# A fourth of eight weight blocks computed as seven products in each pair of FFN chunks

## The reference, cut to what matters

```
v = rmsnorm(h, ffn_norm_w[l])                                # 256 x 2048
h = h + (silu(v @ w_gate[l]) * (v @ w_up[l])) @ w_down[l]    # w_gate, w_up: 2048 x 5632
```

## Time and profile before

| | us |
|---|---|
| median of 3 runs | 2417.15 (2416.17 to 2417.87) |
| profiled execution, its own time | 2416.8 |
| its span | 2415.0 |
| TensorE busy | 2402.1 (99%) |
| VectorE busy | 1652.5 (68%) |
| ScalarE busy | 1324.2 (55%) |
| mean granted clock of TensorE | 0.998 |
| ffn1's ten pairs | 451.6 to 882.8 in the span |

### The profile page before, as it was taken

How to read it: one execution, slowest core, us unless ns; L and a number is a source line. 1 busy time by engine, 2 the same in 40 slices (tenths; PEclk the granted TensorE clock), 3 DMA queues, 4 the chain that set the end, 5 groups by cost and what they waited for, 6 DMA issues and landing times.

```text
span 2415.0 us, 36120 instructions
## 1 busy us (share of the span) xinstructions
PE 2402.1 (99%) x13287; PEld 2030.0 (84%) x13287; DVE 1652.5 (68%) x2053; ACT 1324.2 (55%) x1691; POOL 47.1 (2%) x105
## 2 busy tenths in 40 slices
PE   9999999999999999999999999999999999999999
PEld 8888888788888888888888888898888888888887
DVE  6478765788888885445668575477777777644465
ACT  5467744555555555444655455466656556444464
POOL 2300000000000000000000000000000000000000
PEclk9999999999999999999999999999999999999999
DMA  8644546566666666556665556655656666666654
GB/s 269 189 142 120 150 166 184 165 201 194 201 189 206 191 205 205 191 191 183 171 188 168 174 143 188 192 184 183 200 183 189 192 192 190 208 194 193 211 195 150
DMA packets 235102, 448.55 MB, mean 186 GB/s; under 512 B 14368, under 2 KB 31604, under 8 KB 234480
## 3 DMA queue, kind: packets, MB, share of 16 engines
q1 hardware_dynamic: 231712, 434.83, 57.8%
q0 software_dynamic: 3280, 12.21, 1.6%
HBM read 443.84 MB, written 3.15 MB: 185 GB/s over the span
## 4 chain that ended last, share of the span: by engine, by line
PE 97%; DVE 1%; ACT 1%; issue 0%; DMA 0%; SPq 0%; DVEq 0%; ACTq 0%
PE pg L2636 15%; PE pg L2638 15%; PE pg L2637 15%; PE pt L3193 7%; PE pg L3193 6%; PE pg L3119 5%; PE pg L3121 5%; PE pg L3120 5%; PE pg L3197 3%; PE pt L3197 3%; PE pg L2695 3%; PE pg L2696 3%; PE pg L2697 3%; PE pt L3119 1%; PE pt L3121 1%; PE pt L3120 1%
## 5 line engine op out<-in xcount | busy, mean ns | idle before, releaser
L1584 DVE TENSOR_TENSOR wlo<-raw,whi 128x1024 fp32r<-128x1024 f32 (+3 forms) x783 | 926.1, 1193 | 652.3 <-ACT whi L756 650.3
L756 ACT ACTIVATE whi<-raw 128x1024 fp32r<-128x1024 f32 (+3 forms) x813 | 834.1, 1033 | 869.6 <-PE pg L2638 544.8
L2636 PE MATMUL pg<-whi,FH 128*128 128x512 f32 x696 | 271.4, 390 | 0.7 <-DVE FL L2081 0.7
L2638 PE MATMUL pg<-whi,FL 128*128 128x512 f32 x696 | 270.9, 389 | 0.0
L2637 PE MATMUL pg<-wlo,FH 128*128 128x512 f32 x696 | 270.8, 389 | 0.0
L3193 PE MATMUL pt<-A,whi 128*128 128x512 f32 x704 | 244.8, 391 | 0.0
L3193 PE MATMUL pg<-A,whi 128*128 128x512 f32 x640 | 222.3, 391 | 0.0
L2636 PE MATMUL pg<-whi,A 128*128 128x512 f32 (+1 forms) x576 | 221.1, 384 | 0.0
L2638 PE MATMUL pg<-whi,A 128*128 128x512 f32 (+1 forms) x576 | 217.7, 378 | 0.0
L2637 PE MATMUL pg<-wlo,A 128*128 128x512 f32 (+1 forms) x576 | 217.5, 378 | 0.0
L3197 PE MATMUL pg<-A,wlo 128*128 128x256 f32 x704 | 197.3, 280 | 0.0
(11 more groups left out here) (602 smaller groups left out, 4077.8 us busy)
## 6 DMA issues: line engine op xcount, KB each, us to landing
raw<-w_up SPq DMA_DIRECT2D x264, 512.0 KB, 4.4
raw<-w_down SPq DMA_DIRECT2D x176, 512.0 KB, 3.7
raw<-w_in SPq DMA_DIRECT2D x151, 512.0 KB, 3.7
raw<-w_gate SPq DMA_DIRECT2D x88, 512.0 KB, 3.7
raw<-w_out SPq DMA_DIRECT2D x64, 512.0 KB, 3.7
raw<-w_ple_gate SPq DMA_DIRECT2D x32, 512.0 KB, 4.4
raw<-w_in SPq DMA_DIRECT2D x32, 388.0 KB, 3.3
raw<-w_in SPq DMA_DIRECT2D x16, 280.0 KB, 3.2
```

Of the source, the lines that this page charges most:

```text
L756: A(whi[:, n % RING, 0:w], raw[:, n % RING, 0:w], ACT.Copy).then_inc(hi_ready, 1)
L1584: V.tensor_tensor(wlo[:, n % RING, 0:w], raw[:, n % RING, 0:w], whi[:, n % RING, 0:w].bitcast(F32), ALU.subtract).then_inc(lo_ready, 1)
L2636: mm(o, xh, wh, start=first and k == 0, stop=False)
L2638: ins = mm(o, xl, wh, start=False, stop=last and k == SK - 1)
```

## The change

Block 5 becomes a block of seven products, so that 4, 5 and 6 are three such blocks in a row. Sixteen small activation sums are made in place of twelve, four differences in place of five, and the combinations are 24 tiles in place of 22. The hooks that make them move to earlier steps of the first pair.

```diff
-SEVEN = (2, 4, 6)
+SEVEN = (2, 4, 5, 6)
 ScalarE:
-            ffn1({2: f1_in(3), 4: norm_ffn1, 6: lambda: take_root(2, D), 14: f1_combos})
+            ffn1({2: f1_in(3), 4: norm_ffn1, 6: lambda: take_root(2, D), 12: f1_combos})
 VectorE:
-            ffn1({2: f1_in(3), 4: norm_ffn1, 6: lambda: rstd(2, D), 9: f1_whole, 10: f1_differences, 12: f1_seven_sums, 15: f1_combos})
+            ffn1({2: f1_in(3), 4: norm_ffn1, 6: lambda: rstd(2, D), 7: f1_whole, 9: f1_differences, 10: f1_seven_sums, 13: f1_combos})
```

## The result

| | before | after |
|---|---|---|
| median | 2417.51 (4 runs) | 2501.02 (2500.43 to 2502.39, 4 runs) |
| ratio to before, 95% interval | | 1.0346 (1.0333 to 1.036) |
| profiled execution, its own time | 2416.8 | 2501.6 |
| its span | 2415.0 | 2499.7 |
| mean granted clock | 0.998 | 0.987 |

The account below looks back on a forecast made before the run. The prediction took TensorE to bound the kernel, busy for 99% of the span. To the profiled 2416.8 us it added -6.8 + 67.6 - 6.0 + 22 = +76.8, giving 2493.6 us, forecast as 2494, range 2463 to 2522.

Parts of the forecast that it names:

- Matmuls removed: Block 5 on TensorE goes from 24 to 21 matmuls in each of 10 pairs, all on the path: -6.8 us.
- The wait of the three in a row: TensorE waits for the shared T set before blocks 5 and 6, 20 times 3.38 us: +67.6 us.
- Start of the pairs: Earlier sums remove the XL gap and slow matmuls, less a new 0.7 us gated-product wait: -6.0 us.
- The clock: Granted clock falls in half of the 20 new TensorE gaps, slowing matmuls behind them: +22 us, ends 0 and +44.
- The clock never falls: Rival 1: the new gaps stay too short to lower the clock, 2471.6 us; chance 0.21.
- In each gap: Rival 2: the clock falls in every one of the new gaps, 2515.6 us; chance 0.19.
- Only one transition stalls: Rival 3: only one of block transitions 4 to 5 and 5 to 6 waits, 2437.8 us, up to 2449; chance 0.06.
- faster: Rival 4: the wait before block 5 is hidden and TensorE does not stop, 2404.0 us; chance 0.03.
- The busy share in the pairs: Sign in the new profile: TensorE's busy share in ffn1 near 87%.
- The slow matmuls: Sign in the new profile: 128x512 matmuls of more than 0.39 us in blocks 5, 6 and 7.

Follow-up runs that it names:

- the kernels with two and three blocks of seven: Against the changed kernel, seven products only in blocks 2 and 4 (2417.7 us) or in 2, 4 and 6 (2412.0 us), hooks early in both.
- Filled gaps: Changed kernel with 12 idle matmuls on TensorE ahead of block 5 and of block 6 in each pair: 2472.73 us, ratio 1.0229.
- scattered sevens: Changed kernel with seven products in blocks 2, 4 and 6 as before, only the hooks at their new, earlier steps: 2412.0 us, ratio 0.9975.
- one pair of neighbours: Changed kernel with seven products in blocks 2, 4 and 5 instead of 2, 4, 5 and 6, hooks early: 2458.87 us, ratio 1.0167.
- the first half gets another home: Changed kernel with the first two weight sums and their low parts alternating between two homes: 2471.93 us, ratio 1.0222.
- when they go back: Changed kernel, four blocks of seven products, with the hooks back at their old steps: 2507.15 us, ratio 1.0365.
- low parts first: Changed kernel with VectorE making the low parts wlo before waiting for the T set, and TensorE's start waiting for these alone: 2436.68 us, ratio 1.008.
- the short filling: Changed kernel with 4 idle matmuls, in place of the filled gaps' 12, ahead of blocks 5 and 6: 2495.7 us, ratio 1.0325.

## Why the prediction was right

Forecast 2494, measured 2501.0, inside 2463 to 2522; the direction and the likeliest case are those forecast.

- *Matmuls removed, -6.8.* Priced at 6.3 us by the kernels with two and three blocks of seven, within some 3 us. Right as far as this can tell; that 240 more matmuls in the gaps cost nothing shows the other side of it, that a matmul counts only where TensorE does not wait.
- *The wait of the three in a row, +67.6.* Twenty waits of 3.1 us, in the line forecast, with restarts 3.29 us late where 3.28 was forecast. Filled gaps less scattered sevens is 2472.7 - 2412.0 = 60.7 us, and that is to be 67.6 - 6.8 = 60.8. The mechanism is shown from four sides: it comes with neighbours and not with work (one pair of neighbours, ten waits), it shrinks by 0.9 us when the first half gets another home, it nearly goes when the low parts are made first, and it does not depend on the clock.
- *Start of the pairs, -6.0.* Measured -6.2 with the hooks alone, and +6.1 when they go back. The wait of 0.7 us on the gated product, counted from the end of the stream, was 0.67.
- *The clock, +22.* Measured 28.3 (2501.0 - 2472.7). This is the one term that I sized too small: I took half of the gaps, which was a choice between two ends and read from no row, and it fell in 13 of 20. The price of a fall, 2.2 us read from the single one before, is met by the mean, 28.3 / 13 = 2.2, but by no fall: six cost 2.7 us and seven 1.5, and that this mix gives the same mean is luck. Where all falls were short, as with one pair of neighbours, the price was 1.5. In the changed kernel the clock mostly falls at the first gap of a pair (9 of 10). Behind each of the six long stretches the second gap was spared (rows above, 1.00 behind 598.69); behind each of the three short ones it was not.
- *The parts together.* -6.2 + 60.7 + 28.3 = 82.8, against 83.5 measured; the difference is that of the two medians of the kernel before, 2418.22 and 2417.51.
- *Rivals.* "The clock never falls" (2471.6) is what the filled gaps made of it, 2472.7: a good number for a kernel that was not this one. "In each gap" (2515.6) falls with the seven gaps without a fall. "Only one transition stalls" and "faster" fall with the 20 waits. The rule of the Trainium skill (TensorE: Matmul & The Clock Gate, "Why this matters for your kernels") that idle gaps between bursts of matmuls bring the clock down, which I had applied to every gap, agrees with the trace in its direction only: 13 of 20.
- *Not forecast.* The busy share in the pairs (87% by full clock) reads 45.14 / 51.38 = 88%, since slow matmuls count as busy. The slow matmuls stand in blocks 5 and 6; in block 7, where I expected some too, there are none.

## What to carry to other kernels

Price a saving in matmuls by the column of elementwise work that feeds them: here 30 matmuls less (7 us) took away the cover of a 4.3 us column that can start only when a shared buffer is released, and two such waits in each pair cost ten times as much (68 us). Ask of each buffer what is queued in strict order behind its wait; making first what does not need it returned 64 of 84 us without another byte. Count a gap on TensorE twice where it is long, here 2.4 us and more, as the wait and as the slower matmuls that may follow (in 11 to 13 of 20 gaps here, and in 9 of 10 with one pair of neighbours). Move preparation earlier where it is a wait of its own: that part alone is a faster kernel, 2412.0 us.

## What the runs showed of the hardware

- Idle matmuls made the kernel faster: 240 of them, 28.3 us, by keeping the granted clock at 1.00.
- Gaps in which the clock fell were short: 13 falls in 20 gaps of 3.3 us, 9 in 10 of them with one pair of neighbours, 12 in 20 of 2.4 us behind four idle matmuls, 11 in 20 of 2.4 us without these. In 20 gaps of 0.6 us (filled) and in 20 of 0.9 to 1.6 us (low parts first) there was none.
- A fall is not of one length: 65 us at the lower level for 13 falls in the changed kernel (six of 6.8 and seven of 3.4), 30.7 for 9 with one pair of neighbours and 41 for 12 with the short filling (3.4 each). What decides between them was not tried.
- Of a long stretch 2.7 us were lost behind the gap, of a short one 1.5. Where it fell well before the end of the gap, as in the kernel before (at 453.8, with the gap ending at 455.97), part of the stretch passed while TensorE stood idle anyway.
